# An expert loop of 12 steps instead of 13: three experts in two steps, on array columns in pieces of 64 and 32

## The reference

```python
def _moe(h, w_router, b_router, w_gate, w_up, w_down):
    scores = jax.nn.softmax(h @ w_router, axis=-1)
    sel = scores + b_router
    # the best of 4 groups of experts, and in it the best two experts of the token
    _, idx = lax.top_k(masked, TOP_K)
    wts = chosen / jnp.sum(chosen, axis=-1, keepdims=True)
    for e in range(N_EXPERTS):
        act = jax.nn.silu(h @ w_gate[e]) * (h @ w_up[e])      # 1024 -> 512
        y += combine[..., e:e + 1] * (act @ w_down[e])         # 512 -> 1024
    return y
```

## Time and profile before

| | |
|---|---|
| median of 3 runs | 1396.0 us (1395.11 to 1398.91) |
| the profiled execution | 1394.58 us, of which the span from first to last instruction is 1393.0 |
| PE busy | 1125.0 us, 81% of the span |
| VectorE, ScalarE, GpSimd busy | 411.6, 238.2, 189.0 us |
| DMA | 360.67 MB, mean 259 GB/s over the span |
| PE in the lines of B steps (L889) | 290.9 + 143.1 us busy |
| PE in the lines of P steps (L891) | 86.4 + 42.5 us busy |

### The profile page before, as it was taken

The page is one execution under the profiler, slowest core; times in us unless marked ns, Lnnn a source line. Parts: engine busy times, 40 slices in busy tenths (PEclk is TensorE's granted clock), DMA queues, the critical chain, the costliest instruction groups (busy, mean ns, idle before and its releaser), DMA issues.

```text
span 1393.0 us, 12312 instructions
## 1 busy us (share of the span) xinstructions
PE 1125.0 (81%) x4632; PEld 541.5 (39%) x4632; DVE 411.6 (30%) x880; ACT 238.2 (17%) x499; POOL 189.0 (14%) x322
## 2 busy tenths in 40 slices
PE   3898189999999919999977985589708999999990
PEld 0455044444443414445543542344404444344340
DVE  3545700000000064362165652123560101000005
ACT  2121010000000022221125651111201001000001
POOL 6100210000000030000118631010030000000002
PEclk8987689999999959999997998799858999999995
DMA  9999778999998941132423019865335899998925
GB/s 365 379 421 377 302 224 339 422 361 373 426 336 346 378 144 54 61 103 84 172 77 108 1 34 357 291 204 234 140 130 195 348 424 346 383 420 315 373 105 207
DMA packets 57210, 360.67 MB, mean 259 GB/s; under 512 B 7300, under 2 KB 7796, under 8 KB 39149
## 3 DMA queue, kind: packets, MB, share of 16 engines
q1 hardware_dynamic: 35712, 285.79, 52.1%
q0 software_dynamic: 19904, 73.58, 15.3%
q10 hardware_dynamic: 1532, 0.49, 0.1%
HBM read 330.26 MB, written 34.29 MB: 262 GB/s over the span
## 4 chain that ended last, share of the span: by engine, by line
PE 72%; DMA 9%; DVE 9%; POOL 4%; issue 3%; ACT 2%; SPq 1%; ACTq 0%; POOLq 0%; DVEq 0%
PE pb L889 31%; PE pb L1071 16%; PE pb L891 9%; DMA ring<-in_ada_w_dram 4%; DMA h<-in_ada_w_dram 3%; PE pb L800 2%; POOL ring L764 2%; PE pb L883 2%; PE pb L830 2%; PE pb L1020 1%; DVE h L1845 1%; POOL xs_d L668 1%; PE pb L1163 1%; PE pb L918 1%; PE pb L1075 1%
## 5 line engine op out<-in xcount | busy, mean ns | idle before, releaser
L889 PE MATMUL pb<-ring,h 128*128 128x512 f32 x640 | 290.9, 604 | 19.7 <-DVE h L1845 19.7
L1071 PE MATMUL pb<-ring,hT_raw 128*128 128x512 f32 x512 | 224.7, 596 | 1.3 <-DVE hT_raw L1658 0.8
L889 PEld LDWEIGHTS pb<-ring,h 128*128 128x128 f32 x640 | 120.1, 193 | 163.2 <-issue 163.2
L889 PE MATMUL pb<-ring,hT_raw 128*128 128x512 f32 x320 | 143.1, 600 | 1.5 <-issue 1.5
L1071 PEld LDWEIGHTS pb<-ring,hT_raw 128*128 128x128 f32 x512 | 96.6, 191 | 116.3 <-issue 114.7
L1859 DVE COPY hT_raw<-pb 128x512 f32<-128x512 f32 x26 | 18.0, 692 | 378.7 <-PE pb L889 288.9
L889 PEld LDWEIGHTS pb<-ring,hT_raw 128*128 128x128 f32 x320 | 60.7, 192 | 80.5 <-issue 80.5
L700 POOL DMA_DIRECT2D ys_d<-hT_raw x26 | 14.1, 541 | 574.0 <-DVE hT_raw L1859 574.0
L891 PE MATMUL pb<-ring,h 128*64 128x512 f32 x384 | 86.4, 596 | 5.9 <-DVE h L1845 5.9
L800 PE MATMUL pb<-ring,cT 128*32 128x512 f32 x384 | 53.6, 689 | 29.3 <-DMA ring<-in_ada_w_dram 29.3
L1853 DVE TENSOR_TENSOR h<-pb,h 128x512 f32<-128x512 f32 x26 | 18.0, 692 | 183.6 <-PE pb L889 145.6
(11 more groups left out here) (333 smaller groups left out, 1152.9 us busy)
## 6 DMA issues: line engine op xcount, KB each, us to landing
ring<-in_w_up_dram SPq DMA_DIRECT2D x32, 2048.0 KB, 11.3
ring<-in_w_down_dram SPq DMA_DIRECT2D x32, 2048.0 KB, 11.6
ring<-in_w_gate_dram SPq DMA_DIRECT2D x32, 2048.0 KB, 9.7
ring<-in_ada_w_dram SPq DMA_DIRECT2D x16, 2048.0 KB, 10.6
ys_d<-hT_raw POOLq DMA_DIRECT2D x26, 512.0 KB, 10.3
h<-xs_d POOLq DMA_DIRECT2D x20, 512.0 KB, 13.8
ring<-in_kv_ada_w_dram SPq DMA_DIRECT2D x4, 2048.0 KB, 9.9
ring<-in_w_kvf_dram SPq DMA_DIRECT2D x4, 2048.0 KB, 16.0
```

The lines of the kernel that those rows point to most:

```text
L889: return T.matmul(bank[:, :], lhs, rhs[0], start=start, stop=stop)
L1071: last = T.matmul(bank[:, :], hT[:, k, col[t]:col[t] + P], w[:, k * 512:(k + 1) * 512], start=(k == 0), stop=(k == KC - 1))
```

## The change

`PATTERN` becomes "BBPBBPBTTB". Each "T" stands for two steps and three experts. In the first step one expert has up to 96 rows (columns 0 to 95) and the middle expert the first 32 of its up to 64 rows (columns 96 to 127); in the second step the middle expert has its other 32 rows on columns 0 to 31 and the third expert 96 rows on columns 32 to 127. A step's work is now listed in `LANES`: (place, first column, columns, first row of the expert). There are 12 steps: six B, two P, four of T. Six experts have a capacity of 128 rows, four of 96 and six of 64 (before: ten of 128, six of 64).

`tile_product` cuts a lane of 96 columns into a matmul of 64 and one of 32. So a product of a T step is three matmuls: 64, 32, 32 columns in the first step, 32, 32, 64 in the second. `load_x` loads each lane by itself, so two loads in a P or a T step. `units` waits for the weight slots of both lanes. The middle expert's slot is released with the second step. The overflow table has 10 entries instead of 8 (three fill copies instead of two), VectorE's capacities have three values, and GpSimd writes the places' ranks and rows with 32 memsets instead of 26 iotas.

```diff
-    PATTERN = "BBPBBBPBBBPBB"
-    NSTEP = len(PATTERN)
+    NOV = 10
+    PATTERN = "BBPBBPBTTB"
+    CAPS = (P, 96, HALF)
+    LANES, PLACE_CAP, PLACE_ROW, PLACE_STEP = [], [], [], []
+    for kind in PATTERN:
+        q, n = len(PLACE_CAP), len(LANES)
         if kind == "B":
+            LANES.append([(q, 0, P, 0)])
...
+        elif kind == "P":
+            LANES.append([(q, 0, HALF, 0), (q + 1, HALF, HALF, 0)])
...
+            LANES.append([(q, 0, 96, 0), (q + 1, 96, 32, 0)])
+            LANES.append([(q + 1, 0, 32, 32), (q + 2, 32, 96, 0)])
+            PLACE_CAP += [96, HALF, 96]
+            PLACE_STEP += [n, n + 1, n + 1]
+    NSTEP = len(LANES)
...
-                    for q in STEP_PLACES[n]:
-                        if q + 2 < NE:
+                    for q in range(NE - 2):
+                        if PLACE_STEP[q] == n:
                             refill(kind, q + 2)
...
+            for q in range(NE):
+                link(g.memset(place_rank[:, q:q + 1], float(PLACE_RANK[q])))
+                link(g.memset(place_row[:, q:q + 1], float(PLACE_ROW[q])))
...
-                    for a, q in enumerate(places):
+                    for q, r0, m, first in LANES[n]:
                         off = pool.value_load(tabi[0:1, q:q + 1], min_val=0, max_val=NASSIGN)
-                        g.dma_start(xg[a * m:a * m + m, par, :], xs_d[bass.ds(off, m), :]).then_inc(xg_loaded[par], 16)
+                        g.dma_start(xg[r0:r0 + m, par, :], xs_d[bass.ds(off + first, m), :]).then_inc(xg_loaded[par], 16)
...
-            def tile_product(bank, lhs, rhs, start, stop):
-
-                if len(rhs) == 1:
-                    return T.matmul(bank[:, :], lhs, rhs[0], start=start, stop=stop)
-                for a in range(2):
-                    last = T.matmul(bank[HALF * a:HALF * a + HALF, :], lhs[:, HALF * a:HALF * a + HALF], rhs[a],
-                                    start=start, stop=stop, tile_position=(0, HALF * a))
+            def tile_product(bank, lhs, lanes, cols, start, stop):
+
+                for w, r0, m in lanes:
+                    pieces = {P: [(r0, P)], HALF: [(r0, HALF)], 32: [(r0, 32)],
+                              96: [(0, HALF), (HALF, 32)] if r0 == 0 else [(32, 32), (HALF, HALF)]}[m]
+                    for c0, c in pieces:
+                        last = T.matmul(bank[c0:c0 + c, :], lhs[:, c0:c0 + c], w[:, cols], start=start, stop=stop,
+                                        tile_position=(0, c0))
                 return last
...
-                link(V.tensor_scalar(cap[:, :], order[:, :], NBIG - 0.5, float(-HALF), ALU.is_ge, ALU.mult))
-                link(V.tensor_scalar(cap[:, :], cap[:, :], float(P), None, ALU.add))
+                link(V.tensor_scalar(cap[:, :], order[:, :], FIRST_RANK[1] - 0.5, None, ALU.is_ge))
+                link(V.scalar_tensor_tensor(out=cap[:, :], in0=order[:, :], scalar=FIRST_RANK[2] - 0.5, in1=cap[:, :],
+                                            op0=ALU.is_ge, op1=ALU.add))
+                link(V.tensor_scalar(cap[:, :], cap[:, :], -32.0, float(P), ALU.mult, ALU.add))
```

More of the change, by code:

```diff
@@ L49, in bass_yoco_stream_step @@
     NASSIGN = 2 * TOK
-    NOV = NASSIGN // P
+    NOV = 10
     XROWS = NASSIGN + P
-    PATTERN = "BBPBBBPBBBPBB"
-    NSTEP = len(PATTERN)
+    PATTERN = "BBPBBPBTTB"
     HALF = P // 2
[L57 to L61, removed]
+    CAPS = (P, 96, HALF)
+    LANES, PLACE_CAP, PLACE_ROW, PLACE_STEP = [], [], [], []
+    for kind in PATTERN:
+        q, n = len(PLACE_CAP), len(LANES)
         if kind == "B":
-            STEP_PLACES.append([q])
+            LANES.append([(q, 0, P, 0)])
+            PLACE_CAP += [P]
+            PLACE_ROW += [n * P]
             PLACE_STEP += [n]
-            PLACE_ROW += [n * P]
-            PLACE_RANK += [big]
-            big += 1
-        else:
[L69 to L73, removed]
+        elif kind == "P":
+            LANES.append([(q, 0, HALF, 0), (q + 1, HALF, HALF, 0)])
+            PLACE_CAP += [HALF, HALF]
+            PLACE_ROW += [n * P, n * P + HALF]
+            PLACE_STEP += [n, n]
+        else:
+            LANES.append([(q, 0, 96, 0), (q + 1, 96, 32, 0)])
+            LANES.append([(q + 1, 0, 32, 32), (q + 2, 32, 96, 0)])
+            PLACE_CAP += [96, HALF, 96]
+            PLACE_ROW += [n * P, n * P + 96, (n + 1) * P + 32]
+            PLACE_STEP += [n, n + 1, n + 1]
+    NSTEP = len(LANES)
+    FIRST_RANK = [sum(c > cap for c in PLACE_CAP) for cap in CAPS]
+    PLACE_RANK = [FIRST_RANK[CAPS.index(c)] + PLACE_CAP[:q].count(c) for q, c in enumerate(PLACE_CAP)]
     YROWS = NSTEP * P + NOV * P
@@ L214, in bass_yoco_stream_step @@
         ovs = sb("ovs", [P, NE])
-        e16 = sb("e16", [P, 4, NE])
+        e16 = sb("e16", [P, 2, NE])
         gmul = gainb[:, :].rearrange("p (a n) -> p a n", a=2)
@@ L246, in bass_yoco_stream_step @@
         kns = stage[:, 1, 128:192].rearrange("p (a t) -> p a t", a=2)
-        ind = bandf[:, 1104:1104 + 3 * NOV * NE].rearrange("p (a j e) -> p a j e", a=3, j=NOV)
+        ind = bandf[:, 1056:1056 + 3 * NOV * NE].rearrange("p (a j e) -> p a j e", a=3, j=NOV)
         qbd = stage[:, 0, :].rearrange("p (j a q) -> p j a q", j=NPAIR, a=2)
@@ L674, in load_x @@
                     par = (layer * NSTEP + n) % 2
-                    places = STEP_PLACES[n]
-                    m = P // len(places)
-                    for a, q in enumerate(places):
+                    for q, r0, m, first in LANES[n]:
                         off = pool.value_load(tabi[0:1, q:q + 1], min_val=0, max_val=NASSIGN)
-                        g.dma_start(xg[a * m:a * m + m, par, :], xs_d[bass.ds(off, m), :]).then_inc(xg_loaded[par], 16)
+                        g.dma_start(xg[r0:r0 + m, par, :], xs_d[bass.ds(off + first, m), :]).then_inc(xg_loaded[par], 16)
                 pool.wait_ge(scattered, 16 * 2 * NT * (layer + 1))
@@ L901, in pe_gate @@
                             pe.wait_ge(E.silu, g)
-                    last = tile_product(pb[3], xgT[:, par, k, :], [w[:, k * DE:(k + 1) * DE] for w in ws],
-                                        k == 0, k == KC - 1)
+                    last = tile_product(pb[3], xgT[:, par, k, :], ws, slice(k * DE, (k + 1) * DE), k == 0, k == KC - 1)
                 if ks[-1] == KC - 1:
@@ L910, in pe_up @@
                 for k in range(KC):
-                    last = tile_product(pb[4], xgT[:, par, k, :], [w[:, k * DE:(k + 1) * DE] for w in ws],
-                                        k == 0, k == KC - 1)
+                    last = tile_product(pb[4], xgT[:, par, k, :], ws, slice(k * DE, (k + 1) * DE), k == 0, k == KC - 1)
                 last.then_inc(E.up, 1)
@@ L927, in pe_down @@
                         c0 = k * D + 512 * half
-                        last = tile_product(pb[5 + half], hactT[:, k, :], [w[:, c0:c0 + 512] for w in ws],
-                                            k == 0, k == KE - 1)
+                        last = tile_product(pb[5 + half], hactT[:, k, :], ws, slice(c0, c0 + 512), k == 0, k == KE - 1)
                     last.then_inc(E.down, 1)
@@ L935, in units @@
                 def units(first, n):
-                    for q in STEP_PLACES[n]:
+                    for q, r0, m, _ in LANES[n]:
                         pe.wait_ge(slot_loaded[first + q % 2], 16 * (before[first + q % 2] + q // 2 + 1))
-                    return [ring[:, first + q % 2, :] for q in STEP_PLACES[n]]
+                    return [(ring[:, first + q % 2, :], r0, m) for q, r0, m, _ in LANES[n]]
                 def tokens(n):
                     g = b + n
-                    loads = sum(len(STEP_PLACES[i % NSTEP]) for i in range(g % 2, g + 1, 2))
+                    loads = sum(len(LANES[i % NSTEP]) for i in range(g % 2, g + 1, 2))
                     pe.wait_ge(xg_loaded[g % 2], 16 * loads)
@@ L1803, in places @@
                 scan(ovs[:, :], ovc[:, :])
[L1805 to L1808, removed]
+                link(V.tensor_scalar(e16[:, 0, :], ovs[:, :], float(P), float(NSTEP * P), ALU.mult, ALU.add))
+                tt(e16[:, 0, :], e16[:, 0, :], cap[:, :], ALU.subtract)
+                tt(e16[:, 0, :], e16[:, 0, :], base[:, :], ALU.subtract)
+                tt(e16[:, 1, :], offs[:, :], cap[:, :], ALU.add)
                 tt(selv[:, :, :], rank[:, :, :], bc(cap[:, :], NT, 1), ALU.is_ge)
-                tt(selv[:, :, :], selv[:, :, :], bc(e16[:, 1, :], NT, 1), ALU.mult)
+                tt(selv[:, :, :], selv[:, :, :], bc(e16[:, 0, :], NT, 1), ALU.mult)
                 tt(selv[:, :, :], selv[:, :, :], bc(base[:, :], NT, 1), ALU.add)
@@ L1824, in places @@
                 tt(ind[one_row, 0, :, :], ind[one_row, 0, :, :],
-                   e16[one_row, 2, :].unsqueeze(1).to_broadcast([1, NOV, NE]), ALU.add)
+                   e16[one_row, 1, :].unsqueeze(1).to_broadcast([1, NOV, NE]), ALU.add)
                 tt(ind[one_row, 0, :, :], ind[one_row, 0, :, :], ind[one_row, 1, :, :], ALU.mult)
```

## The result

The changed kernel takes 1550.74 us (median of 4 runs, 1550.33 to 1551.31) against 1395.95 (1395.11 to 1398.91): ratio 1.1107, interval 1.1091 to 1.1123, so 155 us slower. Its profiled execution took 1550.46 us, with a span of 1548.7.

What follows compares the result with a forecast made beforehand. TensorE was taken to bound the kernel (72% of the chain). Removed work -48.9, T products +215.3 and interrupted runs +3.1 give +169.5 us, from 1396.0 to 1565 us; range 1532 to 1600, holding 0.80.

Steps and rivals of the forecast that it cites:

- The step on which all rests: TensorE in T products: a piece of another width waits until the array is empty, wherever its columns lie; +215.3 us.
- The price of a T product: Three matmuls on TensorE take 1.98 us, +1.12 against a B product; +26.9 us a T step, +215.3 over eight.
- The missed term: Edges between T-step matrices: the forecast counted only interrupted runs of T products, one extra width change each, +3.1 us.
- Removed work and free work: Expert loops: one step and one P's changes fewer per layer, -48.9 us; weight loads, table, constants and copies cost nothing.
- rival 1: T products: pieces of different width stream side by side, 1352 us plus 5 for transfers, 1357 us; chance 0.13.
- The clock: TensorE's granted clock, 0.99 of 2.4 GHz before; a fall in T steps, half the columns idle, would make the forecast wrong.

Runs made afterwards that it cites:

- the mix without T: Kernel before the change, with the second expert's 64 columns in P steps cut into two matmuls of 32 beside the first's 64; 1551.34 us, ratio 1.111.
- control: Kernel before the change, with both experts' 64 columns in P steps cut into two matmuls of 32, four per product; 1394.04 us, ratio 0.9994.

## Why the prediction was right, point by point

- **The step on which all rests held.** That a piece of another width waits, wherever its columns lie, was read from one gap of 0.18 us at two like places; that is thin, and the prediction itself left 0.13 to the rival. One width for all (1374) and the mix without T (1551, control 1394) show it as the cause. That the array runs empty in between remains a reading of the 0.09 us between the last record of one width and the first of the other. The runs agree with the sentence of the Trainium skill that the prediction weighed (TensorEngine Tiling (Array Packing), Tiling Modes: a change of the tiling mode drains the engine); by the other sentence alone the mix would have cost as little as the control.
- **The price of a T product held.** Put together from the earlier trace rows as 1.98 us, it measures 1.985 (starts at 371.492, 371.972, 372.494, 372.948 and 373.477: 0.480, 0.522, 0.454, 0.529). Records of one width and a change of width were read at two other places in the program, and added up.
- **The missed term.** The steps were to be 50 us and the loops 85 us longer; they are 48.5 to 48.6 and 79. The prediction let each run of T products that is broken off pay one change more (3.1 us in all) and did not lay the order 64, 32, 32 of one step against the 32, 32, 64 of the other, by which equal widths meet on free columns in six places a layer. That is 11 us less, shown by the run with the widest piece first: there the steps are 50.43 us, the loops are 85.0 and 83.3 longer than before, and the kernel takes 1564 (1559.15 to 1566.63), where 1565 was predicted. By that spread, the agreement to 1 us is in part luck.
- **Removed work and free work held.** No weight wait stands in the T steps, and the DMA share came to 0.74 and 0.67 where 0.7 was predicted. The added loads, copies and constants show nowhere in the changed kernel: PE's waits in its expert lines are those of before. With one width and half refills, which has them all, PE's time is 1351.1, where rival 1 had 1352 ahead of its transfers. The reading that no wait but the copy's stands in the expert lines was not quite so: twice 0.7 us ahead of the last down is there too, before and after, and changes nothing.
- **The clock held:** 0.99, with half of the columns idle at any time.
- **Rival 1's price was too low, though the case did not come up.** Short T steps would have given 1357 by its working, 1352 for PE and 5 for transfers. One width makes them short: PE's part holds (1351.1 with half refills), the transfers cost 23. The rival saw one pair per layer late by a fraction of its 16.6 us landing; in fact both pairs wait 3.0 to 3.5 in each layer, the fill copies add 5.8, and the lower clock comes on top (6.2 us in three ups).
- **What stays open:** the 2.4 us outside the loops. Runs of the kernel before alone spread over more (1392.9 to 1399.1), and no run was aimed at it.

## What to carry to other kernels

Pieces that are to stream beside each other want one width: cut everything to the narrowest (four 32s cost what one 128 does here), rather than to the fewest pieces. This is shown here for 64 and 32 columns of fp32. Where widths must change, count the changes and put equal widths at both sides of an edge; a table of each matrix's first and last record, with the distance to the next, shows at once where that happens. And once TensorE's part is short, see what the transfers allow before its whole gain is booked: neither the other order of steps nor the one other place for the copies gave a gain here, since each moved a wait to where other transfers stood.

## What the runs showed of the hardware beyond that

- Records of one matrix began beside the last ones of the matrix before where width was equal and columns were free; with widths sorted, the next matrix started 1.28 us ahead of the last record of the one before (391.55 against 392.83).
- A change of width inside a stream cost 0.134 us, averaged over both directions: 0.09 to 0.10 until the first record of the new width, and 0.03 to 0.05 by which that record takes longer.
- Behind waits of nearly one length the granted clock went different ways: after one of 3.06 us it was 0.50 for some 6 us, and an up took 10.0 us instead of 7.1; after two of 3.00 and 3.09 us, in layer 0 of the same execution, it stayed at 1.00.
